# The last expert item finished by slot: gated item rows, early sums of all tokens, one scatter at the end

## The reference

```python
logits = (t @ router_w).astype(jnp.float32)
top_v, top_i = lax.top_k(logits, TOP_K)          # TOP_K = 2 of N_EXPERTS = 8
gates = jax.nn.softmax(top_v, axis=-1)
for e in range(N_EXPERTS):
    w_e = jnp.sum(jnp.where(top_i == e, gates, 0.0), axis=-1)
    out = out + w_e[:, None] * swiglu(t, w1[e], w3[e], w2[e]).astype(jnp.float32)
...
x = x + gt2 * f          # gt2: one row for the prompt, one for each of the 8 sequences
...
y_prompt = rmsnorm(xp, final_g)
y_sample = rmsnorm(xs, final_g)
```

## Time and profile before

| | |
|---|---|
| median of three runs | 1541.12 us (1540.0 to 1542.54) |
| profiled execution | 1537.92 us, of which the span is 1535.9 us |
| busy share of the span | PE 99%, DVE 77%, ACT 62%, POOL 6% |
| DMA | 492.59 MB, 321 GB/s over the span |
| granted clock of the tensor engine | 0.996 of full speed |

### The profile page before, as it was taken

One profiled execution on the slowest core, in us unless ns is written; L12 is line 12 of the kernel. 1 busy time (PEld: TensorE's weight loads), 2 busy tenths in 40 slices (PEclk: granted clock), 3 DMA queues, 4 the chain that ended last, 5 costly groups with the idle time before them and its releaser, 6 DMA issues.

```text
span 1535.9 us, 21793 instructions
## 1 busy us (share of the span) xinstructions
PE 1517.2 (99%) x8105; PEld 1292.5 (84%) x8105; DVE 1189.3 (77%) x971; ACT 946.0 (62%) x723; POOL 94.7 (6%) x133
## 2 busy tenths in 40 slices
PE   8999999999999999999999999999999999999997
PEld 5787999999988888888888888888888888888885
DVE  4686444444476869888898888888888888889997
ACT  3454423332344567777777777777777777778774
POOL 3210000000002023000000000000000000001001
PEclk9999999999999999999999999999999999999998
DMA  9997944444447869999999999999999999999993
GB/s 360 386 352 280 364 151 150 138 163 138 162 176 302 256 213 352 357 394 401 368 375 390 383 372 386 379 381 382 382 377 388 382 372 374 378 373 369 401 399 124
DMA packets 235378, 492.59 MB, mean 321 GB/s; under 512 B 10155, under 2 KB 16171, under 8 KB 231226
## 3 DMA queue, kind: packets, MB, share of 16 engines
q1 hardware_dynamic: 227110, 472.82, 83.7%
q0 software_dynamic: 5920, 18.57, 3.2%
q10 hardware_dynamic: 2308, 0.64, 0.2%
HBM read 481.86 MB, written 10.36 MB: 320 GB/s over the span
## 4 chain that ended last, share of the span: by engine, by line
PE 96%; DVE 2%; ACT 1%; DMA 1%; issue 0%; POOL 0%; SPq 0%; POOLq 0%; ACTq 0%
PE ps L1784 20%; PE ps L1786 20%; PE ps L1785 20%; PE ps L2200 4%; PE ps L2202 4%; PE ps L2201 4%; PE ps L1812 2%; PE ps L2210 2%; PE ps L2212 2%; PE ps L2211 2%; PE ps L2348 2%; PE ps L2154 1%; PE ps L2156 1%; PE ps L2155 1%; PE ps L1998 1%; PE ps L1829 1%
## 5 line engine op out<-in xcount | busy, mean ns | idle before, releaser
L1138 DVE TENSOR_TENSOR w_lo<-raw,w_hi 128x2048 fp32r<-128x2048 f32 x366 | 835.4, 2291 | 172.4 <-ACT w_hi L762 171.0
L762 ACT ACTIVATE w_hi<-raw 128x2048 fp32r<-128x2048 f32 x366 | 701.6, 1918 | 258.3 <-PE ps L1786 159.5
L1784 PE MATMUL ps<-w_hi,split 128*128 128x512 f32 x1392 | 549.7, 395 | 0.6 <-DVE w_lo L1138 0.5
L1786 PE MATMUL ps<-w_hi,split 128*128 128x512 f32 x1392 | 543.3, 390 | 0.0
L1785 PE MATMUL ps<-w_lo,split 128*128 128x512 f32 x1392 | 542.6, 390 | 0.0
L1784 PEld LDWEIGHTS ps<-w_hi,split 128*128 128x128 f32 x1392 | 261.6, 188 | 58.5 <-DVE w_lo L1138 4.3
L1786 PEld LDWEIGHTS ps<-w_hi,split 128*128 128x128 f32 x1392 | 261.4, 188 | 55.1
L1785 PEld LDWEIGHTS ps<-w_lo,split 128*128 128x128 f32 x1392 | 261.8, 188 | 51.8
L2200 PE MATMUL ps<-split,w_hi 128*128 128x320 f32 x432 | 134.0, 310 | 0.0
L2202 PE MATMUL ps<-split,w_lo 128*128 128x320 f32 x432 | 133.7, 309 | 0.0
L2201 PE MATMUL ps<-split,w_hi 128*128 128x320 f32 x432 | 133.7, 309 | 0.0
(11 more groups left out here) (368 smaller groups left out, 1304.5 us busy)
## 6 DMA issues: line engine op xcount, KB each, us to landing
raw<-in_moe_w SPq DMA_DIRECT2D x336, 1024.0 KB, 7.4
raw<-in_ffn_w SPq DMA_DIRECT2D x42, 1024.0 KB, 5.1
raw<-in_ada_w SPq DMA_DIRECT2D x40, 1024.0 KB, 8.6
raw<-in_w_in SPq DMA_DIRECT2D x12, 1024.0 KB, 9.2
raw<-in_ada_w SPq DMA_DIRECT2D x16, 512.0 KB, 11.3
raw<-in_w_out SPq DMA_DIRECT2D x8, 1024.0 KB, 10.6
item_rows<-plain POOLq DMA_DIRECT2D x12, 512.0 KB, 7.8
plain<-in_x_prompt SPq DMA_DIRECT2D x2, 512.0 KB, 3.8
```

Of the source, the lines that this page charges most:

```text
L762: a.activation(w_hi[:, (s0 + j) % SPL], raw[:, (u0 + j) % RAW], ACT.Copy).then_inc(hi_ready, 1)
L1138: v.tensor_tensor(w_lo[:, (s0 + j) % SPL], raw[:, (u0 + j) % RAW], w_hi[:, (s0 + j) % SPL].bitcast(F32), ALU.subtract).then_inc(lo_ready, 1)
L1784: t_.matmul(out, a_hi, b_hi, start=first_, stop=False)
L1786: return t_.matmul(out, a_lo, b_hi, start=False, stop=last_)
```

## The change

**In the first item.** The places are no longer sorted. The two gates are computed in `find_places`, and the one-hot matrix that gives each slot its token now carries a second set of columns with the slot's gate; the product `item_tokens` is 28 columns wide where it was 14. `slot_table` writes token numbers (counted from 1, so that 0 is an empty slot) and gates per slot. SyncE copies the nine gt2 rows into a table `gt2_rows` in memory.

**At the end of each item but the last,** ScalarE copies the item's output with the slot's gate as scale, so `item_rows` holds gated rows. ScalarE now also waits at the head of each item for its own last copy (`y_cp`).

**In the last item.** ScalarE's loop over steps is written out, and VectorE's is a loop again. GpSimd first works out, for each of the last item's 128 slots, its token, its sequence and its row in each output, by some 14 small operations. It gathers both places of block 0, then gt2 by slot, which it multiplies by the slot's gate (`end_gt2`). After units 6 and 14 it gathers blocks 1 and 2, and for each block it adds the two places, multiplies by gt2, adds x (`total`), and stores the sum to `part_rows`. The tokens of the last item find zeros at that place, so these are all tokens' sums without the last item. It then gathers the partial rows of the last item's slots (`end_part`). ScalarE squares each block's sum behind steps 3, 4 and 5, and GpSimd multiplies it by the final gain. At the end of the item ScalarE takes the three roots, VectorE the reciprocals, ScalarE scales, and SyncE stores all blocks. Rows of tokens of the last item lack its part in these stores, and are written again behind them.

**Behind the last product.** VectorE multiplies each half of the output in PSUM by `end_gt2`, adds `end_part`, and the 128 rows get their norm by slot. GpSimd waits for these rows and for the three stores, and writes the rows by two indirect DMAs, one for the prompt's output and one for the samples', in which slots that belong to the other (or to none) have a number out of bounds and are skipped.

```diff
+        sp.dma_start(d['gt2_rows'].rearrange("r (k c) -> k r c", c=P),
+                     d['mod_rows'][2].rearrange("(k r) c -> k r c", r=ROWS)).then_inc(gt2_rows_in, 16)
...
-            sp.dma_start(dst, y1[b][0:n]).then_inc(y_stored, 16)
+            sp.dma_start(dst, y0[b][0:n]).then_inc(y_stored, 16)
...
         gp.wait_ge(y_cp, last_item + 1)
         gp.dma_start(d['item_rows'][bass.ts(last_item - 1, P), :], e_y).then_inc(y_out, 16)
...
+        step(g.tensor_copy(slot_now[:], slot_tab[:, :, bass.ds(last_item, 1)]))
...
+        def fetch_outputs(b):
             n = BLK[b]
+            for j, y in enumerate((y0, y1)):
+                gp.indirect_dma_start(y[b][0:n], None, d['item_rows'],
+                                      bass.IndirectOffsetOnAxis(ap=posi[0:n, j, b:b + 1], axis=0)).then_inc(y_early[b], 16)
+
+        def total(b):
+
+            n = BLK[b]
+            gp.wait_ge(y_early[b], 32)
+            step(g.tensor_tensor(y0[b][0:n], y0[b][0:n], y1[b][0:n], ALU.add))
+            step(g.tensor_tensor(y0[b][0:n], y0[b][0:n], (gt2p if b < 2 else gt2s)[0:n], ALU.mult))
+            g.tensor_tensor(y0[b][0:n], y0[b][0:n], x_tok[0:n, b, :], ALU.add).then_inc(y_tot, 1)
+            gp.wait_ge(y_tot, b + 1)
+            gp.dma_start(d['part_rows'][b * P:b * P + n, :], y0[b][0:n]).then_inc(part_out, 16)
...
+        fetch_outputs(0)
+        gp.wait_ge(gt2_rows_in, 16)
+        gp.indirect_dma_start(end_gt2, None, d['gt2_rows'],
+                              bass.IndirectOffsetOnAxis(ap=seq_idx[:, 0:1], axis=0)).then_inc(last_gt2, 16)
...
+        g.tensor_scalar(end_gt2, end_gt2, slot_now[:, 1, :], None, ALU.mult).then_inc(gt2_gated, 1)
         for b in range(1, NBLK):
-            gp.wait_ge(lo_ready, n_items * N_FFN + (S_MOE - 46 + 12 * b))
+            gp.wait_ge(lo_ready, n_items * N_FFN + (S_MOE - 44 + 8 * b))
             g.nop().then_inc(steps_done, 1)
             gp.wait_ge(steps_done, b)
-            fetch_outputs(b, 0, y0, y_early)
...
+            fetch_outputs(b)
+            total(b - 1)
+        total(NBLK - 1)
+        gp.wait_ge(part_out, 16 * NBLK)
+        gp.indirect_dma_start(end_part, None, d['part_rows'],
+                              bass.IndirectOffsetOnAxis(ap=idx_now[:, 0:1], axis=0)).then_inc(part_in, 16)
+        gp.wait_ge(fg_in, 16)
         for b in range(NBLK):
-            fetch_outputs(b, 1, y1, y_in)
+            n = BLK[b]
+            gp.wait_ge(y_sq, b + 1)
+            g.tensor_tensor(y0[b][0:n], y0[b][0:n], fgain[0:n], ALU.mult).then_inc(y_gained, 1)
+        gp.wait_ge(end_done, 2)
+        gp.wait_ge(y_stored, 16 * NBLK)
+        for j, (dst, n) in enumerate(((o[0][0], NP_TOK), (o[1].rearrange("b t d -> (b t) d"), NS_TOK))):
+            gp.indirect_dma_start(dst, bass.IndirectOffsetOnAxis(ap=out_idx[:, j:j + 1], axis=0), end_rows, None,
+                                  bounds_check=n - 1, oob_is_err=False).then_inc(end_out, 16)
+        gp.wait_ge(end_out, 32)
...
     @block.scalar
...
+            act.wait_ge(y_cp, i + 1)
             e_up(2)
...
+            if last:
+                for s in range(1, NSTEP):
+                    e_middle(s)
+                    b = s - 3
+                    if 0 <= b < NBLK:
+                        n = BLK[b]
+                        act.wait_ge(y_tot, b + 1)
+                        a.activation(y1[b][0:n], y0[b][0:n], ACT.Square, accum_out=y_ss[0:n, b:b + 1]).then_inc(y_sq, 1)
...
-            a.activation(e_y[:, 0:B], ps[:, 3, :], ACT.Copy)
+            a.activation(e_y[:, 0:B], ps[:, 3, :], ACT.Copy, scale=gate_now[:])
...
+        act.wait_ge(y_rec, 1)
+        for b in range(NBLK):
             n = BLK[b]
+            act.wait_ge(y_gained, b + 1)
+            a.activation(y0[b][0:n], y0[b][0:n], ACT.Copy, scale=y_rs[0:n, b:b + 1]).then_inc(y_done, 1)
+        for c in range(2):
+            act.wait_ge(end_sum, c + 1)
+            a.activation(e_silu[:], end_rows[:, c * B:(c + 1) * B], ACT.Square,
+                         accum_out=end_ss[:, c:c + 1]).then_inc(end_std, 1)
...
+        act.wait_ge(end_rec, 1)
+        act.wait_ge(end_gained, 1)
+        a.activation(end_rows[:, 0:B], e_g[:], ACT.Copy, scale=end_rs[:, 0:1]).then_inc(end_done, 1)
...
     @block.vector
...
+            ve.wait_ge(exp_done, 1)
+            v.tensor_tensor(item_id[:, :, 0, :], at_least[:, :, 0:NI + 2], at_least[:, :, 1:NI + 3], ALU.subtract)
+            step(v.tensor_scalar(dsum[:], etop[:], 1.0, None, ALU.add))
+            step(v.reciprocal(gate[:, 0], dsum[:]))
+            step(v.tensor_tensor(gate[:, 1], etop[:], gate[:, 0], ALU.mult))
...
         for c in range(2):
             cols = slice(c * B, (c + 1) * B)
...
+            ve.wait_ge(split_used, n_items * N_FFN + (S_MOE - 1 + c))
+            step(v.tensor_tensor(end_rows[:, cols], ps[:, 3 + c, :], end_gt2[:, cols], ALU.mult))
+            ve.wait_ge(part_in, 16)
+            v.tensor_tensor(end_rows[:, cols], end_rows[:, cols], end_part[:, cols], ALU.add).then_inc(end_sum, 1)
+            if c == 0:
+                ve.wait_ge(end_sum, 1)
+                ve.wait_ge(fg_in, 16)
+                v.tensor_tensor(e_g[:], end_rows[:, cols], fgain[:, cols], ALU.mult).then_inc(end_gained, 1)
+        ve.wait_ge(end_std, 4)
+        v.reciprocal(end_rs[:], end_sd[:]).then_inc(end_rec, 1)
...
     @block.tensor
...
-        for b in range(NBLK):
-            n = BLK[b]
-            pe.wait_ge(y_in[b], 16)
...
-                ins = t_.matmul(ps[0:n, LAST_BANK[b][c], :], sel, ey_lo[:, cols], start=False, stop=True)
-            ins.then_inc(last_mm, 1)
```

More of the change, by code:

```diff
@@ L244, in write_program @@
       thr, tokid, at_least, item_id, item_no, slot_no,
-      idx_f, posi_f, dsum, y_ss, y_sd, y_rs, later, sooner, place, part, y_gate)) = views(
+      idx_f, posi_f, dsum, y_ss, y_sd, y_rs)) = views(
         "plain", F32,
@@ L389, in write_program @@
     y_free = sem("y_free")
[L390 to L397, removed]
+    last_gt2 = sem("last_gt2")
+    gt2_rows_in = sem("gt2_rows_in")
+    gt2_gated = sem("gt2_gated")
+    gate_cp = sem("gate_cp")
+    items_out = sem("items_out")
+    y_tot = sem("y_tot")
+    y_sq = sem("y_sq")
+    y_gained = sem("y_gained")
+    y_rec = sem("y_rec")
+    part_out = sem("part_out")
+    part_in = sem("part_in")
+    end_sum = sem("end_sum")
+    end_gained = sem("end_gained")
+    end_std = sem("end_std")
+    end_rec = sem("end_rec")
+    end_done = sem("end_done")
+    end_out = sem("end_out")
     y_early = [sem(f"y_early{b}") for b in range(NBLK)]
-    y_in = [sem(f"y_in{b}") for b in range(NBLK)]
     steps_done = sem("steps_done")
-    y_sum = sem("y_sum")
     y_std = sem("y_std")
@@ new lines, in _ @@
+        step(g.tensor_scalar(in_seq[:], seq_from[:], token, None, ALU.is_le))
+        for half in (NSEQ // 2, NSEQ // 4, NSEQ // 8):
+            step(g.tensor_tensor(in_seq[:, 0:half], in_seq[:, 0:half], in_seq[:, half:2 * half], ALU.add))
+        step(g.tensor_copy(seq_idx[:], in_seq[:, 0:1]))
+        for j, below_ in enumerate((1, NP_TOK + 1)):
+            step(g.tensor_scalar(out_no[:, j:j + 1], token, below_ - 0.5, 4096.0, ALU.is_lt, ALU.mult))
+            step(g.tensor_tensor(out_no[:, j:j + 1], out_no[:, j:j + 1], token, ALU.add))
+            step(g.tensor_scalar(out_no[:, j:j + 1], out_no[:, j:j + 1], -float(below_), None, ALU.add))
@@ L1044, in _, with e_item @@
         xs_split_hi(1, XS_BANK0)
-        def e_item(i, last):
+        def e_item(i, last, first=False):
             def e_up(j, s=None):
@@ L1066, in e_item, with e_middle @@
             e_up(4)
-            with act.Fori(1, NSTEP) as s:
+            def e_middle(s):
                 for j in range(1, 4):
@@ L1646, in extra_items @@
             v.tensor_copy(table[:, 0:EXTRA_MAX], tab[:, 0:EXTRA_MAX]).then_inc(routed, 1)
[L1648 to L1663, removed]
-            if q % 2 == 0:
-                ve.wait_ge(y_early[b], 16)
-                ve.wait_ge(xtok_cp, NBLK)
-                step(v.scalar_tensor_tensor(out=y0[b][0:n], in0=y0[b][0:n], scalar=y_gate[0:n, 0, b:b + 1],
-                                            in1=(gt2p if b < 2 else gt2s)[0:n], op0=ALU.mult, op1=ALU.mult))
-            else:
-                step(v.tensor_tensor(y0[b][0:n], y0[b][0:n], x_tok[0:n, b, :], ALU.add))
         def e_item(i, last, first=False):
@@ L1701, in e_item @@
             e_mul(None)
-            if last:
-                for s in range(1, NSTEP - 1):
-                    e_step(s)
-                    early_part(s - 1)
-                    e_lo_unit(5, s)
-            elif first:
+            if first:
                 for s in range(1, NSTEP - 1):
@@ L1745, in _ @@
[L1745 removed]
+        ve.wait_ge(y_std, 1)
+        v.reciprocal(y_rs[:, 0:2], y_sd[:, 0:2])
+        v.reciprocal(y_rs[0:NS_TOK, 2:3], y_sd[0:NS_TOK, 2:3]).then_inc(y_rec, 1)
+        ve.wait_ge(gt2_gated, 1)
         for c in range(2):
             cols = slice(c * B, (c + 1) * B)
[L1748 to L1759 removed]
```

(3 more changed lines are left out.)

145 lines of the change are left out of this document (59 added, 86 removed).

## The result

The changed kernel takes 1551.03 us (median of six, 1549.25 to 1553.99) against 1541.12: ratio 1.0066, 95% interval [1.0056, 1.0077], 9.9 us slower. The forecast of 1540.5 was too low by 10.5 us, the range ended at 1549; of the rivals it is (B), VectorE as the bound, 1 us above its upper end. One slow execution of before, at 5389 us, is left out. The profiled execution is at 1549.66 with a span of 1547.9.

A forecast was written before the change was run, and what follows sets the result against it. The tensor engine bounds until the last product, then an 18.0 us end. -7.9 end, +6 moved work, +0.5 DMA, +0.8 first item: -0.6 us, forecast median 1540.5; own range 1537.5 to 1544.5, with rivals 1532 to 1549.

The forecast's parts named there:

- (B): Last item: VectorE becomes the bound from 1426 on, if moved work costs over 9.7 us; 1545 to 1550; chance 0.21.
- The end: Behind the last product: 18.0 us long before, gain 7.9 us, with indirect writes landing after 4.8.
- The moved work: Last item: GpSimd's two-operand operations hold VectorE 1.58 us each; +6 us taken, outer bounds 0 and +18.
- the prediction's own formula: Last item: bunched holds less 1.0 us run-ahead and 0.28 idle per unit; 12.5, without today's 1.6 +10.9.
- cover by PSUM products: Last item: VectorE's PSUM reads, 6.3 us between 1420 and 1497, may absorb holds; +10.9 falls to +4.6.
- 1.6 for those additions: Last item: the additions removed from VectorE now cost the tensor engine six waits, 1.6 us together.
- its 1546.5: Last item: with the skill page's 2.25 us per GpSimd operation, holds 6 us more; sum +5.4, time 1546.5.
- The rows of the second mixer: Trace rows of 704- and 480-column GpSimd sums, extrapolated at 1.65 ns per column to a 1.58 us hold.
- What holds it: Last item: VectorE and GpSimd take turns where both read two SBUF operands; PSUM products probably not held.
- DMA: Last item: +3390 KB of transfers make weight units 2 to 3 us late; +0.5 us taken, 0 to +5.
- First item: Five more small operations between the places and GpSimd's comparison, 0.17 to 0.25 each: +0.8 us.
- ScalarE: Items before the last: scaled copies and the wait at an item's head cost 0, at most +1 over six items.

The follow-up runs named there:

- e6: The changed kernel without GpSimd's twelve sum and gain operations and without the added transfers of the last item: 1534.08 us, 0.9950 of before.
- e5: The changed kernel with GpSimd's twelve 128x1024 operations reading one operand (times a constant) instead of two: 1538.47 us, 0.9980 of before.
- e1: The changed kernel without GpSimd's nine operations of the totals and three of the gains, every transfer kept: 1540.52 us, 1.0002 of before.
- e3b: The changed kernel with the nine operations of the totals on VectorE, transfers and gains left on GpSimd: 1540.43 us, 1.0003 of before.
- e4b: The changed kernel with gate operations out of find_places, one step later, and ScalarE's copy wait just before overwriting gate_now: 1551.56 us, 1.0063 of before.
- e10: e9 with the second gather of each block adding on the way, so seven operations on VectorE, not ten: 1537.40 us, 0.9981 of before.
- e9: The changed kernel with totals and gains on VectorE, gathers spread evenly, part stores late, e4b's edits: 1536.07 us, 0.9976 of before.

## Why the prediction was wrong, step by step

**The end: right, in part by luck.** 8.2 gained, 7.9 forecast, with errors inside that nearly cancel: GpSimd began the first indirect write 1.0 us after the rows were ready (I had 0), the writes landed after 3.0 us, not 4.8, and the span ended some 0.8 after that, not 0.4.

**The moved work: wrong, and this decides.** The step that failed is "1024 columns hold VectorE 1.05 + 320 x 1.65 ns = 1.58 us", and with it the choice of +6 "near the lower end". The hold is 2.2 us. Put into the prediction's own formula it gives 5.0 + 10.8 + 3.1 + 0.9 = 19.8 us without cover by PSUM products and 13.5 with it; measured are 16.1. The PSUM products were no cover of 6.3 us: only three of them fall in a GpSimd turn, as the one at 1468.40, and the splits are 24.6 us longer where twelve holds of 2.2 make 26.4. Net of what the removed additions cost (e6 is 9.1 below before in the last stage, 8.2 of it the end, so 0.9) the term is +15.2 and not +6. I had 1.6 for those additions, but that row is of weight loads; the products lost nothing there by the earlier trace rows. Rival (B) had the mechanism and named the point, holds of 2.0 us; it was given 0.21. The Trainium skill's GPSIMD Engine Reference, section Performance versus the Vector engine, from which I had worked out 2.25 us (an estimate, half of its time for 2048 columns), is confirmed here at 2.2; its 1546.5 was nearer than the forecast, and fell short by 3 us in this term, since the PSUM cover was taken whole. The rows of the second mixer were no scale for this: two operations of other widths, and a line through two points drawn to half as many columns again. There GpSimd ends 1.7 ns a column after VectorE's operation does, here 2.2; why isn't settled.

**What holds it: right.** Two SBUF operands on both sides: e5 takes one away on GpSimd's, and a hold falls from 2.2 to 0.4 us in the mean; the PSUM products have one less on VectorE's, and stay at 0.68. That is what the Trainium skill's SBUF — State Buffer, section SBUF: two separate sides, says of VectorE's side. Of GpSimd's it asks only that the operation reads SBUF; how much its second operand weighs, e5 shows.

**DMA: too low, and hidden by the holds.** +0.5 was forecast; behind the held splits it is 2.0 in the last stage (0.75 by the medians), and by the two timelines not through late weights but through GpSimd's gains, which the transfers pushed together. That a late tensor engine asks for weights later, as argued, no run shows. By itself it is 6.7, above the bound of 5, with 1.6 of it the clock behind a wait, which the prediction left out: take the holds away and this is the next limit (e1, e3b).

**First item: right, ScalarE: wrong by 1.** find_places takes 0.9 us longer (0.8 forecast, from five more operations where the trace has four). The items between cost 1.0 together, where I took 0 with a bound of 1; about half is the wait at the head of an item (e4b).

The sum of what was measured: -8.2 + 15.2 + 2.0 = +9.0 in the last stage, +0.9 and +1.0 ahead of it. The remaining 1.1 of the 12.0 between the two spans lies ahead of the first item. At 478.36 the two executions are level; then a run of 48 products (line 2311 before, 2350 after) takes 7.74 us in after, with the clock at its lower level from 560.0 to 563.4, behind waits of 0.8 and 0.7 us for VectorE, and 6.21 before, where the lower level (554.8 to 558.2) had passed. At 576 after is 1.0 behind. So this part is the clock's and not the change's, as far as two executions can show.

## What to carry to other kernels

Where VectorE is the next bound, a two-operand operation on GpSimd is not work taken off it: here 1024 columns cost VectorE 2.2 us of standing still, and the same operation on VectorE itself 1.22. Price such a move by the nearest full-size row or the worst bound, and look twice at any extrapolation that makes the move pay. A term that is small because another delay covers it must be priced again before that delay is taken away: the transfers were 2 us behind the held splits and 6.7 without them.

## What the runs showed that I had not expected

A lone hold is not free: three, a step apart, cost 1.0 us each (3.0), where the prediction had 0.3 for one alone, and twelve 1.3 each (16.1). And an indirect gather that adds on the way slows the weights beside it: ScalarE waited 11.9 us for them in e10 and 1.1 in e9, with the gathers issued at the same splits. The clock, too, moves single executions by several us and must be read first: e4b's first store stands 4.6 us later than after's.
